# One unit later for the weight loads of the attention stages, and low halves two pieces behind in the forgetting attention

## The reference

```python
# first block, FoX: o = softmax(q k^T / sqrt(d) + F_t - F_s) v
s = jnp.einsum('bhqd,bhkd->bhqk', qb, kh) + Fb[..., None] - F[:, :, None, :]
s = jnp.where(kpos[None, :] <= qpos[:, None], s, -jnp.inf)
o = jnp.einsum('bhqk,bhkd->bhqd', jax.nn.softmax(s, axis=-1), vh)
...
# second block: latent attention, then the attention over indexed keys
y_a = mla_attention(q_nope, q_pe, k_nope, k_pe, v_a, pos) * silu(z_a)
y_b = dsa_attention(q_b, k_b, v_b, q_idx, k_idx, w_idx, rel_bias, pos, topk) * silu(z_b)
merged = sigmoid(gate_a) * (y_a @ w_o_a) + sigmoid(gate_b) * (y_b @ w_o_b)
x = x + merged @ w_out
```

## Time and profile before

| what | before |
|---|---|
| median of 3 runs | 1103.9 us (1103.29 to 1106.97) |
| the profiled execution | 1105.54 us, of which its span is 1103.7 us |
| TensorE busy | 1056.7 us, 96% |
| VectorE, ScalarE, GpSimd busy | 612.5, 461.1 and 252.2 us |
| mean granted clock of TensorE | 0.983 |

### The profile page before, as it was taken

The page is one execution under the profiler, slowest core; times in us unless marked ns, Lnnn a source line. Parts: engine busy times, 40 slices in busy tenths (PEclk is TensorE's granted clock), DMA queues, the critical chain, the costliest instruction groups (busy, mean ns, idle before and its releaser), DMA issues.

```text
span 1103.7 us, 13481 instructions
## 1 busy us (share of the span) xinstructions
PE 1056.7 (96%) x5152; PEld 849.2 (77%) x5160; DVE 612.5 (55%) x1049; ACT 461.1 (42%) x808; POOL 252.2 (23%) x155
## 2 busy tenths in 40 slices
PE   7989999999999999999999998899999999999996
PEld 6868787677888888888888776777887766788885
DVE  6584367757444433454445466898756664425544
ACT  6426345545323221222234465555755444423322
POOL 1362332222111100001014333322322322321100
PEclk9998899999999999999999999999999998999998
DMA  8111142212332232222332426211213323122322
GB/s 288 62 58 59 39 117 83 73 58 77 103 108 94 98 115 96 77 96 96 99 112 77 127 61 211 77 58 58 91 61 99 91 92 103 59 95 96 99 74 77
DMA packets 34799, 102.32 MB, mean 93 GB/s; under 512 B 4560, under 2 KB 8032, under 8 KB 34736
## 3 DMA queue, kind: packets, MB, share of 16 engines
q1 hardware_dynamic: 34736, 101.47, 28.1%
HBM read 93.35 MB, written 4.74 MB: 89 GB/s over the span
## 4 chain that ended last, share of the span: by engine, by line
PE 73%; DVE 14%; ACT 6%; issue 4%; SPq 2%; DMA 1%; POOL 1%; DVEq 0%; ACTq 0%; POOLq 0%
PE bank L1373 20%; PE bank L1377 20%; PE bank L1375 20%; PE bank L1507 2%; PE bank L1498 2%; DVE m L2073 1%; DVE score L2075 1%; PE bank L1387 1%; DVE score L2064 1%; PE bank L1388 1%; PE bank L1389 1%; ACT WH L1559 1%; PE bank L1479 1%; DVE small L1957 1%; DVE f_s L1861 1%
## 5 line engine op out<-in xcount | busy, mean ns | idle before, releaser
L1373 PE MATMUL bank<-HH,WH 128*128 128x512 f32 x808 | 330.0, 408 | 7.8 <-ACT HH L1567 5.9
L1377 PE MATMUL bank<-HH,WL 128*128 128x512 f32 x808 | 318.5, 394 | 0.0
L1375 PE MATMUL bank<-HL,WH 128*128 128x512 f32 x808 | 318.4, 394 | 0.0
L2156 POOL TENSOR_TENSOR WL<-WS,WH 128x1024 fp32r<-128x1024 f32 x64 | 154.9, 2420 | 367.8 <-ACT WH L1559 367.2
L1373 PEld LDWEIGHTS bank<-HH,WH 128*128 128x128 f32 x808 | 154.5, 191 | 43.7 <-ACT WH L1563 5.8
L1559 ACT ACTIVATE WH<-WS 128x1024 fp32r<-128x1024 f32 x161 | 167.8, 1049 | 41.9 <-PE bank L1377 41.0
L1377 PEld LDWEIGHTS bank<-HH,WL 128*128 128x128 f32 x808 | 153.6, 190 | 33.6
L1375 PEld LDWEIGHTS bank<-HL,WH 128*128 128x128 f32 x808 | 154.1, 191 | 29.4 <-issue 0.5
L1810 DVE TENSOR_TENSOR WL<-WS,WH 128x1024 fp32r<-128x1024 f32 x97 | 126.4, 1310 | 34.2 <-ACT WH L1559 34.1
L2204 POOL TENSOR_TENSOR fa<-fa,fg 128x512 f32<-128x512 f32 x22 | 28.3, 1286 | 273.4 <-DVE fa L2010 273.4
L1373 PE MATMUL bank<-GH,WH 128*128 128x512 f32 x176 | 68.5, 389 | 0.0
(11 more groups left out here) (335 smaller groups left out, 1736.2 us busy)
## 6 DMA issues: line engine op xcount, KB each, us to landing
WS<-wall SPq DMA_DIRECT2D x161, 512.0 KB, 3.4
scratch<-rows SPq DMA_DIRECT2D x8, 320.0 KB, 5.3
X<-xT SPq DMA_DIRECT2D x8, 256.0 KB, 6.5
b_t<-scratch SPq DMA_DIRECT2D x8, 256.0 KB, 3.8
outT<-X SPq DMA_DIRECT2D x8, 256.0 KB, 2.1
b_m<-b_m SPq DMA_DIRECT2D x11, 128.0 KB, 4.3
f_s<-f_s SPq DMA_DIRECT2D x8, 128.0 KB
f_m<-f_m SPq DMA_DIRECT2D x8, 128.0 KB
```

The lines of the kernel that those rows point to most:

```text
L1373: e.matmul(b[:, :], wh, xh[:, at_k, :], start=k == 0, stop=False)
L1375: e.matmul(b[:, :], wh, xl[:, at_k, :], start=False, stop=False)
L1377: m = e.matmul(b[:, :], wl, xh[:, at_k, :], start=False, stop=k == n - 1)
L2156: e.tensor_tensor(WL[:, u % NW, :], WS[:, u % NST, :], f32(WH[:, u % NW, :]), ALU.subtract).then_inc(*tick(w_low_g, u))
```

## The change

There are two edits. First, the step `split` carries a number `ahead`. It is 3 (`NST`) until the step list comes to the woven stretch that holds the latent and the index attention, and 2 from there on. `load` now keeps its own count of units and issues all up to the one that it is asked for. So from that point the load of unit n stands at the step `split` of unit n-2 rather than n-3 in SyncE's queue. It still waits for the low half of unit n-3, and for nothing new. At the step of unit u the queue now waits for the low half of unit u-1, where it waited for that of unit u. Second, in `fox_stack` the low half of a piece comes two pieces behind its high half instead of one, so a pair takes six steps instead of five; the pair still counts as ready after both lows of its first head.

```diff
-        now = {"low": w_low_v, "due": 0.0, "per": 0.0, "product": None}
+        now = {"low": w_low_v, "due": 0.0, "per": 0.0, "product": None, "ahead": NST}
...
-                do("split", u=u)
+                do("split", u=u, ahead=now["ahead"])
...
-            for n in range(5):
+            for n in range(6):
                 if n < 4:
                     do("stack_high", p=p, i=i, hl=parts_of[n][0], what=parts_of[n][1], free=free)
-                if n > 0:
-                    do("stack_low", p=p, i=i, hl=parts_of[n - 1][0], what=parts_of[n - 1][1], free=free)
-                if n == 2:
+                if n > 1:
+                    do("stack_low", p=p, i=i, hl=parts_of[n - 2][0], what=parts_of[n - 2][1], free=free)
+                if n == 3:
                     fox_in[p] = i
                 yield
...
         now["per"] = 1.4
+        now["ahead"] = NST - 1
         side = mla_side()
...
+            loads = [1]
+
             def load(u):
-                if u < NU:
-                    if u >= NST:
-                        q.wait_ge(split_low(u - NST))
-                    e.dma_start(WS[:, u % NST, :], wall[u]).then_inc(*w_in[u % NST].tick(u))
+
+                while loads[0] <= min(u, NU - 1):
+                    n = loads[0]
+                    loads[0] += 1
+                    if n >= NST:
+                        q.wait_ge(split_low(n - NST))
+                    e.dma_start(WS[:, n % NST, :], wall[n]).then_inc(*w_in[n % NST].tick(n))
...
-                    load(s.get("u", 0) + NST)
+                    load(s.get("u", 0) + s.get("ahead", NST))
```

## The result

The changed kernel takes 1095.0 us (median of 4 runs, 1094.4 to 1095.6), the kernel before 1103.7 us beside it (1103.3 to 1107.0): a ratio of 0.9929, interval 0.9913 to 0.9945. By the ratio this is 7.8 us, between 6.1 and 9.6. The forecast was 1096.0, in a range of 1092.5 to 1101.0. The profiled execution fell from 1105.54 to 1095.55, by 10.0 us. Lines of the changed kernel are 6 higher: L1504 answers to L1498, L1312 to L1306.

What follows compares the result with a forecast made beforehand. TensorE, busy 1056.7 of 1103.7 us, was taken as the bound. FoX 2.6, dsa 1.4 + 2.5 and clock 2.9, less 1.0, took 1105.54 to 1097.1; less 1.6 for the median, plus 0.5, gave 1096.0, range 1092.5 to 1101.0.

Steps and rivals of the forecast that it cites:

- these six places: TensorE waits where the change moves something: four in FoX (0.25, 0.83, 1.00, 1.54 us), two in dsa (1.96, 2.49 us).
- FoX, 2.6 us forecast: Moving FoX's low halves later on VectorE shortens TensorE's waits: 1.1 us at pair 1 plus 1.5 at pair 3.
- Pair 3's 1.5: FoX pair 3, TensorE's two waits for scaled row blocks: 0.4 of 1.00 us and 1.1 of 1.54 come back.
- First dsa place, 1.4 forecast: Wait at 887.35 before a head's first logits: the copy no longer stands behind a load; 1.4 of 1.96 us gained.
- that keeps 0.55 us: Behind the 887.35 wait, transposes need a row block whose scale ends on VectorE at 887.70, so 0.55 us of waiting stays.
- Last dsa place, 2.5: Wait at 920.61 before a head's first logits: the copy, without the load, lands sooner; all 2.5 us gained.
- Clock, 2.9: The 6.32 us from 920.61 at half clock run at full clock once the idle time ahead is gone: 2.9 us.
- the rival on the clock: The waits go but the clock loss stays or was not in the median's runs: gain 5.5 us, 1098.4; chance 0.2.
- Loads later, nothing: Weight loads issued up to one unit later in SyncE's queue cost nothing, as 8.5 us of margin stay.
- New small waits, 1.0: TensorE runs closer to the softmax chains, so four new waits of 0.25 us appear: 1.0 us taken off.
- That idle time only changes its place: Rival: GpSimd slows moved low halves and dsa chains still hold TensorE: gain 1 to 3 us, about 1102; chance 0.15.
- A late load: Rival: a weight load comes too late, so ScalarE rounds late and TensorE waits: 1112 us; chance 0.04 with any other loss.

Runs made afterwards that it cites:

- e1: The changed kernel without the later weight loads, so only FoX's low halves are moved: 1099.2 us against 1103.1 for the kernel before, ratio 0.9963.
- e4: FoX as before; loads one unit later from the latent attention on, but back in their old place for the last dsa pair: 1103.1 us, ratio 1.000.
- e6: The kernel before with low halves two pieces behind in FoX's pairs 2 and 3 only, loads as before: 1098.8 us, ratio 0.9967.
- e3: The kernel before with loads one unit later only from the last dsa pair's products on, FoX as before: 1099.3 us, ratio 0.9967.
- e8: The changed kernel with weight loads two units later in the DMA queue instead of one: 1095.4 us, ratio 0.9935 against the kernel before.
- e2: The changed kernel with FoX's low halves as before, so only the loads are moved: 1099.4 us, ratio 0.9957 against the kernel before.
- e5: The kernel before with low halves two pieces behind in FoX's pairs 0 and 1 only, loads as before: 1102.4 us against 1102.8, ratio 0.9998.
- e7: The changed kernel with low halves two pieces behind in all four dsa stacks too: 1093.4 us, ratio 0.9914 against the kernel before.
- e9: The kernel before with low halves two pieces behind in FoX and dsa, loads as before: 1099.6 us against 1103.7, ratio 0.9964.

## Why the prediction was right, term by term

- **Where the time was.** Right in the main: idle time at these six places and the clock behind the last. It left out 0.9 us at pair 2's low halves.
- **FoX, 2.6 us forecast.** In the trace 5.2, as a time 4.1 (e1, which also has the half-clock piece of the latents below). The mechanism was right, sizes were not. Pair 1's 1.1 measured 1.2. Pair 2 had no term and measured 0.9: the forecast counted TensorE's waits from 0.25 us up, and the longest there is 0.18. Pair 3's 1.5 measured 2.9. The step that failed there is "the first still has the low half of `ML` ahead of it, which waits for ScalarE; only ScalarE's exponential in front leaves, so I take 0.4 of 1.00": `MH` itself was late because of the same low half, by way of the maximum and the exponential. "The second loses 1.88 us in front and gets 0.69" was too low in the same way. The upper bound of 2.5 for pair 3 was broken as well, by 0.4 us outside the two brackets: it was made from these alone.
- **First dsa place, 1.4 forecast.** Zero (e4). The wait did go, and the first logits start 6.4 us earlier instead of 4.3. The step "that keeps 0.55 us" was followed for one instruction only. At 883.46 the gain was still 1.4 us, but the next links ran through VectorE too, among them a scale that took 1.97 us beside GpSimd: at 890.60 the shift is 4.4 us, 0.15 more than ahead of the place. The bounds of 0 to 1.96 held it.
- **Last dsa place, 2.5.** In the trace 2.6: from a shift of 4.45 us at 907.09 to 7.1 at 913.52. The copy landed in 2.5 us, where 2.2 was taken.
- **Clock, 2.9.** In the trace 3.0: the shift is 7.1 us at 913.52 and 10.1 at 916.92, and between them neither trace has a wait, so only the speed differs. The Trainium skill (TensorE: Matmul & The Clock Gate, Terms) gives 3.2 by its formula, and the measurement agrees within 0.2. But this size belongs to one execution. Of the five later traces with a wait of 2.2 to 2.5 us here, four had the half clock for 3.41 us, which costs about 1.7, and e6 had none. In the trace of before it lasted from 920.11 for 6.83 us. e3's 3.6 us for the wait of 2.5 with its clock fits a term of 1 to 2. So does the granted clock of whole runs: its mean is 0.9852 over 51 runs of before and 0.9857 over ten of the changed kernel, about 0.5 us of 1100 (an estimate), or 2 us with the 1.5 us lost at 707.59 (see the new small waits) added back. The two profiled executions differ by 0.003, some 3 us. So 2.9 was the size in the profile, and too much for a typical run: there the rival on the clock was partly right. The 0.5 that I allowed for it was in the right direction; it may be part of why the profiled execution gained 10.0 and the medians 8.7.
- **Loads later, nothing.** Right, and with a full further unit to spare (e8).
- **New small waits, 1.0.** Apart from 0.67 and 0.76 in dsa, counted above, there was a loss that I had listed as a sign of error: the piece at 707.59. The shift falls from 5.8 us at 706.89 to 4.3 at 727.63, a loss of 1.5. The piece is in all traces with the low halves of pairs 2 and 3 moved but one (8 of 9), and in none of the five in which they stay (before, e2 to e5). The waits ahead of it (1.19 and 1.86 us for `a_q`) are the same with and without. What decides there stays open.
- **Sum.** Traces: 0.5 at the start, 5.2, -1.5, 0.2, 2.6, 3.0: 10.0 us, against a forecast of 9.4 less 1.0. The 0.5 at the start is not of the change. The total was nearer than its parts, and that is luck: FoX was twice as large, the first place empty, and the clock term too large for a typical run.
- **The rivals.** That idle time only changes its place happened at one of the six places, at a price of 1.4 us. GpSimd's slowing of VectorE is there as the Trainium skill states it (SBUF — State Buffer, SBUF: two separate sides): low halves beside `WL` took 1.98 and 2.41 us, much more than the 0.67 us alone. A scale of 128 columns took 1.97 us there and 0.29 alone. The rival was right in so far as the low half of 2.41 us and this scale stand on the chains to the two new waits; e7 removes both waits, and with a scale just as slow. A late load did not come (e8).

## What to carry to other kernels

- When a wait is to be removed, follow the chain behind it until the engines meet again, and not for one instruction. Where two queues are late at one place (here SyncE's and VectorE's), one edit alone can measure as nothing.
- An operation that no one needs yet, in front of a maximum or a scale, can cost more than its own length: what waits for the maximum has others behind it in its own order. Look for the same queue ahead of both inputs before you credit only part of a wait.
- A DMA queue in order holds a ready copy behind a load that can't go. Put the load behind the copy; here there was room for two units.

## What the hardware showed that I had not expected

- A row's busy time hides waiting. TensorE came 3.8 us earlier in e6, where the idle times of before at these places held 2.8 us (0.01, 0.08, 0.18, 1.00 and 1.54).
- The granted clock fell to 0.50 at the last place behind waits of 2.2 to 2.5 us in five traces (before, e1, e4, e5, e9), but not in e6 behind 2.47 us, and in none of the six traces with a wait of 1.5 to 2.0 us at the first place. The length of the wait alone does not decide it. In the latents it fell in some traces and not in others behind the same 1.86 us:

```profile
706.89 0.50 PE L1379 MATMUL bank<-LQH,WH 128*128 128x512 f32 x1 [1.86 <-DVE a_q L2106]
```
```profile
707.80:711.30 3.50, 3.50 (x19) 2.85 (x18) 3.37 (x9) 0.46 (x2) 0.00 (x0) 1.00 0.17 69
```

  The first row is of the changed kernel, with the half clock from 707.59 on; the second is e8's stretch behind its own wait of 1.86 us, at full clock.
- The same copy of 64 rows landed in 2.2 us with no load issued near it, and took 4.3 us as the median of all eight in the trace of before, most of them issued right behind a load.
